# Where an SBUF arena and its parts start: moving the addresses of a three-pass matmul kernel's buffers

## The chip, the cores and the metric

The kernel runs on one core of one Trainium2 chip. The metric is the device time of one execution in microseconds; the time of before is the median of three runs. The profile is of one further execution.

## What is computed

The reference is a stack of two model blocks in float32, on 512 tokens of 1024 features.

```python
def first_block(x, p, ...):                      # DEPTH = 2
    for i in range(2):
        mix = ssd_mixer(x, ...) if i == 0 else hgrn2_mixer(x, ...)   # in-projection, scan over chunks, out-projection
        h = layer_norm(ALPHA * x + mix, ln_g[i, 0], ln_b[i, 0])
        a = relu(h @ w1[i]); h = layer_norm(ALPHA * h + (a * a) @ w2[i], ln_g[i, 1], ln_b[i, 1])
        x = h + sigmoid(h @ w_gate[i]) * (p[i] @ w_proj[i])
    return x
# second block, one layer: x + (concat(mla_attention, memory_attention) * silu(gate)) @ w_out, then rmsnorm
```

w1 is 1024 x 4096 and w2 4096 x 1024, so each of the two MLPs is the largest piece. All projections are products of 512 tokens with 1024 or more features.

## The kernel before, in words

**Arithmetic.** Every large product is made of three passes. An operand is split into a high part, rounded to the fp32r type, and a low part, the difference; TensorE then adds high x high, high x low and low x high into one PSUM bank. The first named operand of a matmul record in the profile is the one that streams (the moving one), the second the one that stands (the stationary one, which a LDWEIGHTS loads): `f_lo,w_hi` streams f_lo over w_hi.

**Stages in order of time.** The SSD mixer by four groups (about 50 to 310 us), its out-projection, MLP 0 (425 to 790), gate 0, the gated recurrence by eight heads (to 1110) with its out-projection, MLP 1 (1200 to 1560), gate 1, the attention layer (to the end). Weights come from HBM in units of 1024 x 512 values as four DMAs on SyncE's queue into one of two slots. ScalarE rounds a unit's slices into w_hi (line 1654, `split_high`), VectorE makes w_lo (line 2432, `split_low`), and TensorE multiplies in `times_parts` (line 907): for each of 8 slices k and 4 blocks c three matmuls of 512 columns, 96 in a unit. Semaphores count the slices; ScalarE may overwrite a slice of w_hi when TensorE is one block on (`blocks_begun`). In the MLP's first product w stands and f streams, in all others of line 907 the activations stand and w streams. Line 702 is `passes`, used by the SSD mixer and others, with in_hi (in fT), in_lo (in res), rings and z_hi (in the arena), x_lo and z_lo (in the slots) and bc_lo (in gb). Line 1081 is the recurrence's projection, 940 the small plain-f32 product with pT, 667 a transpose.

**Memory.** SBUF buffers are allocated one behind the other, each start rounded up to 32 bytes: two slots of 16 KB per partition, res, rn and fT of 16 KB, gb of 8 KB, then the constants, small tiles and pT, then the arena of 29,920 words. The arena is used again in each stage: `carve` hands out views by a running word number, and `part` makes an fp32r tensor at a given word. The parts of the MLP are hid_hi at word 0, f_hi 5632, hid_lo 9728, f_lo 13824, w_hi 17920 and w_lo 22016; all these are multiples of 512 words, 2048 bytes. yT_hi_a, m_hi and first_hi lie in fT.

Of the kernel before, what the change touches and what calls it, by code (L numbers as in the profile page):

```python
# [12 lines left out]
F32R = mybir.dt.float32r  # L13
# [3 lines left out]
P = 128  # L17
T = 512
NT = T // P
D = 1024  # L20
KD = D // P
HALF = 512
NHALF = D // HALF
DEPTH = 2
# [2 lines left out]
RMS_EPS = 1e-5  # L27
EPS = 1e-6
ARENA = 29920
DFF = 4 * D  # L30
KF = DFF // P
PLE = 256
KP = PLE // P
# [17 lines left out]
NMEM = 256  # L51
MT = NMEM // P
# [16 lines left out]
A_CW, A_CB, A_ROWS = 0, TAPS * CONV_BLOCKS, (TAPS + 1) * CONV_BLOCKS  # L69
# [28 lines left out]
    return c  # L98


class Banks:


# [28 lines left out]
def build(nc, x, p, cst, par_a, par_b, w_ssd, w_dt, dt_bias, a_log, d_skip, w_ssd_out, w_hgrn, w_hgrn_out,  # L132
          ln_g, ln_b, w_mlp1, w_mlp2, w_gate, w_proj, mem, pos, w_mla, w_uq, w_ukv, w_mem, w_mla_out, fin_g, out):
    with ExitStack() as ctx:
        def sb(name, shape, dt=F32):
            return ctx.enter_context(nc.sbuf_tensor(name, shape, dt))
# [2 lines left out]
            return ctx.enter_context(nc.semaphore(name))  # L139


        slots = [sb(f"slot{s}", [P, 4096]) for s in range(2)]
        slots_base = nc.sbuf_base - 2 * 4 * 4096
        res = sb("res", [P, NT, D])
# [3 lines left out]
        fT_base = nc.sbuf_base - 4 * KD * T  # L148
        gb = sb("gb", [P, 2, D])
        gb_base = nc.sbuf_base - 4 * 2 * D  # L150
        con = sb("con", [P, C_ALL])
        col_a = sb("col_a", [P, A_ROWS])
        col_b = sb("col_b", [P, B_ROWS])
        eps_h = sb("eps_h", [P, 1])
        pT = sb("pT", [P, DEPTH, KP, T])
        pT_base = nc.sbuf_base - 4 * DEPTH * KP * T
        posi = sb("posi", [P, NT])
        st6 = sb("st6", [P, NT, 2, 6])
        mv = sb("mv", [P, NT, 2])
        ms = sb("ms", [P, NT, 3])  # L160
        arena = sb("arena", [P, ARENA])
        arena_base = nc.sbuf_base - 4 * ARENA
        psum = ctx.enter_context(nc.psum_tensor("psum", [P, 8, HALF], F32))
        tri = con[:, C_TRI:C_TRI + P]
        ones = con[:, C_ONE:C_ONE + P]
# [1 line left out]
        at = [0]  # L167

        def carve(*shape):
            n = int(np.prod(shape))  # L170
            assert at[0] + n <= ARENA, (at[0], n)
            v = arena[:, at[0]:at[0] + n]
            at[0] += n
            if len(shape) == 2:
                v = v.rearrange("p (a b) -> p a b", a=shape[0])
            if len(shape) == 3:
                v = v.rearrange("p (a b c) -> p a b c", a=shape[0], b=shape[1])
            return v


        xdt = carve(NT, HALF)
        xw = carve(NT, HALF)
        xr = carve(NT, HALF)
        zs = carve(NT, HALF)
        prev = carve(NT - 1, HALF)
# [27 lines left out]
        xdt_first, xw_first = 0, 2048  # L213
        dtT = zs[:, 0, :]
        s_par = prev[:, 0, 0:2 * P].rearrange("p (a n) -> p a n", a=2)
        s_p = [arena[:, 26112 + i * NT * PLE:26112 + (i + 1) * NT * PLE].rearrange("p (t n) -> p t n", t=NT)
               for i in range(DEPTH)]
        Mh = rn[:].rearrange("p t d -> p (t d)").rearrange("p (j l) -> p j l", j=S_HPG)
        bc_w = gb[:].rearrange("p a b -> p (a b)").rearrange("p (k n) -> p k n", k=KD)
# [1 line left out]


        def part(name, first, *shape):
            return nc.alloc_sbuf_tensor_at(name, [P, *shape], F32R, offset=arena_base + 4 * first)

        def over(name, base, *shape):
            return nc.alloc_sbuf_tensor_at(name, [P, *shape], F32R, offset=base)
# [2 lines left out]
        bc_lo = over("bc_lo", gb_base, KD, 256)  # L230
        x_lo, z_lo = over("x_lo", slots_base, KD, HALF), over("z_lo", slots_base + 4 * 4096, KD, HALF)
        rings = [part(f"ring{n}", ring_first + n * KD * 256, KD, 256) for n in range(3)]
        z_his = [part(f"z_hi{n}", ring_first + n * KD * 256, KD, HALF) for n in range(2)]
        yT_hi = [over("yT_hi_a", fT_base, KD, T), part("yT_hi_b", 0, KD, T)]
        yT_lo = [part("yT_lo_a", 13824, KD, T), part("yT_lo_b", 9728, KD, T)]
        sums_parts, picks = over("sums_parts", pT_base, T), over("picks", pT_base + 4 * T, S_HEADS)
# [14 lines left out]
        w_hi, w_lo = part("w_hi", 17920, KD, HALF), part("w_lo", 22016, KD, HALF)  # L251
        hid_hi, hid_lo = part("hid_hi", 0, KD, T), part("hid_lo", 9728, KD, T)

        sq = arena[:, 4096:4096 + 3 * T].rearrange("p (a l) -> p a l", a=3)
        sg = arena[:, 9728:9728 + 4096].rearrange("p (t d) -> p t d", t=NT)

        def pp(i, t):

            return pT[:, i, :, :].rearrange("p k l -> p (k l)") if t == NT - 1 else arena[:, 26112 + t * D:26112 + (t + 1) * D]

        first_hi, first_lo = over("first_hi", fT_base, KD, HALF), z_lo

# [60 lines left out]
        ukv_hi, ukv_lo = part("ukv_hi", 17920, KKV, A_HEADS * 2 * NOPE), part("ukv_lo", 22016, KKV, A_HEADS * 2 * NOPE)  # L323
        out_his = [part("out_hi0", 22016, KD, HALF), part("out_hi1", 16384, KD, HALF)]
        branch_lo = part("branch_lo", 0, KD, T)
        mem_tok = arena[:, 0:MT * D].rearrange("p (a b) -> p a b", a=MT)
        memT = arena[:, MT * D:MT * D + KD * NMEM].rearrange("p (a b) -> p a b", a=KD)
        gate = rn


# [1115 lines left out]
        def _(act):  # L1446
# [235 lines left out]
            def projected(stage, i, j):  # L1682

                t, h = j // NHALF, j % NHALF
                b = full(stage, (h, t))
                act.copy(pp(i, t)[:, h * HALF:(h + 1) * HALF], psum[:, b, :]).then_inc(bank_free[b], 1)
# [470 lines left out]
        def _(dve):  # L2157
# [405 lines left out]
            def half_gate(i, h, t):  # L2563

                cols = slice(h * HALF, (h + 1) * HALF)
                wait_taken(dve, f"gate{i}", (h, t))
                dve.wait_ge(res_ready, NT * (2 * i + 1) + t + 1)
                dve.tensor_tensor(sg[:, t, cols], sg[:, t, cols], pp(i, t)[:, cols], ALU.mult)
                dve.drain()
                dve.tensor_tensor(res[:, t, cols], res[:, t, cols], sg[:, t, cols], ALU.add)\  # L2570
                    .then_inc(sig(f"{('ple_first', 'ple_second')[h]}{i}"), 1)
# [585 lines left out]
```

## Time and profile before

| | |
|---|---|
| median of 3 runs | 1894.97 us (1894.18 to 1897.01) |
| span of the profiled execution | 1893.3 us |
| TensorE busy | 1868.5 us, 99% |
| VectorE, ScalarE, GpSimd busy | 1139.9, 921.3, 178.3 us |
| granted TensorE clock, mean | 0.998 |
| DMA | 162.02 MB, 86 GB/s |

The span runs from the first to the last instruction; the time of a run holds a little more. A matmul's record covers its issue, its stream and its drain, so records of one engine overlap, and two matmuls in a row start nearer to each other than a record is long. Names are those of the program's tensors, with buffer numbers left out: `ring` stands for three of them.

### The profile page before, as it was taken

Reading aid. Unit: us, or ns where it says so; the run is one execution under the profiler, and the core shown is the slowest. Engines: PE = TensorE matmul, PEld = TensorE weight load, DVE = VectorE, ACT = ScalarE, POOL = GpSimd, SP = SyncE. Lnnn points to the kernel's source line nnn. Section 1 sums busy time; section 2 is a strip of 40 time slices with the busy share of each in tenths; the row PEclk is TensorE's granted clock in tenths of the full one; section 3 lists DMA queues with packets and bytes.
Section 4 is the critical chain, followed back from the end, with each engine's and each line's share of the span. In section 5 each row is a group of like instructions: output and inputs, shape, how many; then the busy total and the mean of one; then the engine's idle time right before and its main releaser. Section 6 shows DMA issues by size and latency. Waiting matters only on the chain.

```text
span 1893.3 us, 26981 instructions
## 1 busy us (share of the span) xinstructions
PE 1868.5 (99%) x9678; PEld 1573.6 (83%) x9678; DVE 1139.9 (60%) x2013; ACT 921.3 (49%) x1827; POOL 178.3 (9%) x137
## 2 busy tenths in 40 slices
PE   8999999999999999999999999999999999999998
PEld 7787887877888888899999977888888889887986
DVE  5677577548444434557887876634344587456765
ACT  5765765444332323546768655323333364535551
POOL 0201202004000000400101003100000220001100
PEclk9999999999999999999999999999999999999999
DMA  6131214314223322313312124323222222320001
GB/s 199 45 96 42 87 45 153 114 68 156 89 90 113 108 89 89 89 46 90 90 45 67 45 80 143 112 92 117 102 89 89 89 101 92 116 100 1 1 0 45
DMA packets 116738, 162.02 MB, mean 86 GB/s; under 512 B 6085, under 2 KB 57251, under 8 KB 116643
## 3 DMA queue, kind: packets, MB, share of 16 engines
q1 hardware_dynamic: 115347, 156.04, 24.6%
q0 software_dynamic: 1296, 4.72, 0.7%
q8 instruction: 59, 0.97, 0.2%
q14 instruction: 36, 0.29, 0.0%
HBM read 158.64 MB, written 2.10 MB: 85 GB/s over the span
## 4 chain that ended last, share of the span: by engine, by line
PE 92%; DVE 4%; ACT 3%; DVEq 1%; issue 0%; ACTq 0%; DMA 0%; SPq 0%
PE psum L907 52%; PE psum L702 15%; PE psum L1081 8%; PE psum L667 4%; PE psum L1114 3%; PE psum L1344 2%; PE psum L853 1%; PE psum L940 1%; DVE arena L2275 1%; DVE z_lo L2199 1%; PE psum L1001 1%; PE psum L860 1%; PE psum L848 1%; ACT rn L1548 1%; PE psum L1188 0%; ACT arena L1542 0%
## 5 line engine op out<-in xcount | busy, mean ns | idle before, releaser
L2432 DVE TENSOR_TENSOR w_lo<-slot,w_hi 128x512 fp32r<-128x512 f32 x304 | 233.1, 786 | 352.3 <-ACT w_hi L1654 352.2
L1654 ACT CAST w_hi<-slot 128x512 fp32r<-128x512 f32 x304 | 184.5, 620 | 426.9 <-PE psum L907 411.0
L907 PE MATMUL psum<-f_lo,w_hi 128*128 128x512 f32 x528 | 205.8, 390 | 0.0
L907 PE MATMUL psum<-f_hi,w_hi 128*128 128x512 f32 x512 | 200.1, 391 | 1.4 <-DVE f_lo L2480 1.0
L907 PE MATMUL psum<-w_hi,hid_hi 128*128 128x512 f32 x512 | 199.8, 390 | 0.0
L907 PE MATMUL psum<-w_hi,hid_lo 128*128 128x512 f32 x512 | 199.5, 390 | 0.0
L907 PE MATMUL psum<-f_hi,w_lo 128*128 128x512 f32 x512 | 199.5, 390 | 0.0
L907 PE MATMUL psum<-w_lo,hid_hi 128*128 128x512 f32 x512 | 199.4, 390 | 0.0
L3056 POOL TENSOR_TENSOR res<-rn,gb 128x1024 f32<-128x1024 f32 x16 | 46.3, 2892 | 840.1 <-DVE rn L2420 632.6
L907 PEld LDWEIGHTS psum<-f_lo,w_hi 128*128 128x128 f32 x528 | 99.2, 188 | 20.6 <-issue 0.2
L907 PEld LDWEIGHTS psum<-f_hi,w_hi 128*128 128x128 f32 x512 | 96.1, 188 | 22.9 <-DVE f_lo L2480 1.8
L907 PEld LDWEIGHTS psum<-w_hi,hid_hi 128*128 128x128 f32 x512 | 96.2, 188 | 19.9
L907 PEld LDWEIGHTS psum<-w_hi,hid_lo 128*128 128x128 f32 x512 | 96.2, 188 | 19.9
L907 PEld LDWEIGHTS psum<-f_hi,w_lo 128*128 128x128 f32 x512 | 96.2, 188 | 19.9
L907 PEld LDWEIGHTS psum<-w_lo,hid_hi 128*128 128x128 f32 x512 | 96.2, 188 | 19.7
L907 PE MATMUL psum<-w_hi,f_lo 128*128 128x512 f32 (+2 forms) x224 | 83.0, 370 | 0.0
L702 PE MATMUL psum<-in_hi,ring 128*128 128x512 f32 x192 | 77.7, 405 | 0.0
L702 PE MATMUL psum<-in_lo,ring 128*128 128x512 f32 x192 | 75.5, 393 | 0.0
L667 PE MATMUL psum<-con,arena 128*128 128x128 f32 (+1 forms) x486 | 70.4, 274 | 0.4 <-DVE branch_lo L2977 0.3
L2275 DVE SCALAR_TENSOR_TENSOR arena<-psum,col_a,arena 128x511 f32<-128x511 f32 (+2 forms) x72 | 53.4, 748 | 28.7 <-ACT arena L1536 25.1
L1081 PE MATMUL psum<-w_hi,f_hi 128*128 128x256 f32 x224 | 65.7, 293 | 0.0
L667 PEld LDWEIGHTS psum<-con,arena 128*128 128x128 f32 (+1 forms) x486 | 57.7, 146 | 7.4 <-issue 1.9
(388 smaller groups left out, 4385.1 us busy)
## 6 DMA issues: line engine op xcount, KB each, us to landing
slot<-in_w_mlp SPq DMA_DIRECT2D x128, 512.0 KB, 5.7
slot<-in_w_ssd SPq DMA_DIRECT2D x32, 512.0 KB, 5.7
slot<-in_w_hgrn SPq DMA_DIRECT2D x32, 512.0 KB, 6.7
slot<-in_w_ssd_out SPq DMA_DIRECT2D x16, 512.0 KB, 5.9
slot<-in_w_gate SPq DMA_DIRECT2D x16, 512.0 KB, 5.3
gb<-in_w_ssd SPq DMA_DIRECT2D x8, 512.0 KB, 8.3
slot<-in_w_hgrn_out SPq DMA_DIRECT2D x8, 512.0 KB, 5.8
slot<-in_w_mla SPq DMA_DIRECT2D x8, 512.0 KB, 5.4
```

The costliest lines, as they stand in the source:

```text
L667: return pe.transpose(psum[0:mp, b, cols:cols + kp], src, con[0:kp, C_ID:C_ID + kp])
L702: m = pe.matmul(out, a, m_, start=first and n_pass == 0, stop=last and n_pass == 2)
L848: pe.matmul(psum[:, b, :], Btok[:, c, :], xw[:, c, :], start=True, stop=True).then_inc(bank_full[b], 1)
L853: m = pe.matmul(psum[:, b, j * S_P:(j + 1) * S_P], Mh[:, j, c * P:(c + 1) * P], xdt[:, c, j * S_P:(j + 1) * S_P], start=True, stop=True)
L907: m = pe.matmul(psum[:, bank[c], cols or slice(0, width)], a, m_, start=opens and k == 0 and n_pass == 0, stop=closes and k == KD - 1 and ...
L1081: m = pe.matmul(out, a, m_, start=k == 0 and n_pass == 0, stop=k == KD - 1 and n_pass == 2)
L1114: m = pe.matmul(psum[:, b, c * P:(c + 1) * P], a, a, start=True, stop=True)
L1344: m = pe.matmul(psum[:, b, (t - 1) * V_HEAD:t * V_HEAD], probT[:, (t - 1) % 2, c * P:(c + 1) * P], values(c), **first_and_last(c, nk))
L1654: act.copy(w_hi[:, k, :], as_k(slot_of(stage, n))[:, k, :]).then_inc(high_made, 1)
L2275: m = dve.scalar_tensor_tensor(cv[:, n % 3, back:T], psum[:, b, 0:T - back], col_a[:, at_:at_ + 1], cv[:, n % 3, back:T], ALU.mult, ALU.add)
L2432: dve.tensor_tensor(w_lo[:, k, :], as_k(slot_of(stage, n))[:, k, :], w_hi[:, k, :].bitcast(F32), ALU.subtract).then_inc(low_made, 1)
L3056: pool.tensor_tensor(res[:, t, :], rn[:, t, :], gb[:, 0, :], ALU.mult).then_inc(sig("res_scaled"), 1)
```

## The change

The small tiles col_a, posi, st6, mv and ms move to the front of SBUF; pT and then the arena come right behind gb; the constants con, col_b and eps_h go behind the arena. Within the arena, a function `placed` maps a word number to one up to 14 words later, by the table GUARDS, and the arena grows by 14 words. `carve`, `part` and the views written out by hand all use it. As the allocator rounds to 32 bytes, `part` allocates from the multiple of 8 words below and slices. By the table a buffer that starts at word 9728 comes 8 words (32 bytes) later, from 13824 on 12 words (48 bytes), from 22016 on 14 words (56 bytes).

```diff
+GUARDS = ((5632, 0), (9728, 8), (13824, 12), (17920, 12), (22016, 14), (26112, 14))
+ARENA_WORDS = ARENA + GUARDS[-1][1]
+def placed(word):
+    return word + max([guard for first, guard in GUARDS if first <= word], default=0)
+        col_a = sb("col_a", [P, A_ROWS])
+        posi = sb("posi", [P, NT])
+        st6 = sb("st6", [P, NT, 2, 6])
+        mv = sb("mv", [P, NT, 2])
+        ms = sb("ms", [P, NT, 3])
         slots = [sb(f"slot{s}", [P, 4096]) for s in range(2)]
...
         gb = sb("gb", [P, 2, D])
+        pT = sb("pT", [P, DEPTH, KP, T])
+        arena = sb("arena", [P, ARENA_WORDS])
         con = sb("con", [P, C_ALL])
-        col_a = sb("col_a", [P, A_ROWS])
         col_b = sb("col_b", [P, B_ROWS])
         eps_h = sb("eps_h", [P, 1])
-        pT = sb("pT", [P, DEPTH, KP, T])
-        posi = sb("posi", [P, NT])
-        st6 = sb("st6", [P, NT, 2, 6])
-        mv = sb("mv", [P, NT, 2])
-        ms = sb("ms", [P, NT, 3])
-        arena = sb("arena", [P, ARENA])
...
-            v = arena[:, at[0]:at[0] + n]
+            v = arena[:, placed(at[0]):placed(at[0]) + n]
...
         def part(name, first, *shape):
-            return nc.alloc_sbuf_tensor_at(name, [P, *shape], F32R, offset=arena_base + 4 * first)
+            at_, n = placed(first), int(np.prod(shape))
+            whole = nc.alloc_sbuf_tensor_at(name, [P, at_ % 8 + n], F32R, offset=arena_base + 4 * (at_ - at_ % 8))
+            v = whole[:, at_ % 8:at_ % 8 + n]
+            return v.rearrange("p (a b) -> p a b", a=shape[0]) if len(shape) == 2 else v
```

## Rows read from the trace of the kernel before

**Rows 1.** The page: busy time by engine, then the chain by engine and line.
```profile
PE 1868.5 (99%) x9678; PEld 1573.6 (83%) x9678; DVE 1139.9 (60%) x2013; ACT 921.3 (49%) x1827; POOL 178.3 (9%) x137
...
PE 92%; DVE 4%; ACT 3%; DVEq 1%; issue 0%; ACTq 0%; DMA 0%; SPq 0%
PE psum L907 52%; PE psum L702 15%; PE psum L1081 8%; PE psum L667 4%; PE psum L1114 3%; PE psum L1344 2%; PE psum L853 1%; PE psum L940 1%; DVE arena L2275 1%; DVE z_lo L2199 1%; PE psum L1001 1%; PE psum L860 1%; PE psum L848 1%; ACT rn L1548 1%; PE psum L1188 0%; ACT arena L1542 0%
```
**Rows 2.** Waits of TensorE: total us, times, longest.
```profile
PE psum L667 <- DMA rn<-in_x: 5.7, 2, 5.4
```
**Rows 3.** Timeline, TensorE, 800 to 804 us: start, us, instruction (19 matmuls).
```profile
800.12 0.39 PE L907 MATMUL psum<-w_lo,f_hi 128*128 128x512 f32 x1
...
804.20 0.39 PE L907 MATMUL psum<-w_lo,f_hi 128*128 128x512 f32 x1
```
**Rows 4.** Timeline of the weight loads, same stretch.
```profile
800.12 0.19 PEld L907 LDWEIGHTS psum<-w_hi,f_lo 128*128 128x128 f32 x1
```
**Rows 5.** Timeline, TensorE, MLP 0's second product (14 matmuls).
```profile
499.96 0.39 PE L907 MATMUL psum<-w_hi,hid_lo 128*128 128x512 f32 x1
...
502.90 0.39 PE L907 MATMUL psum<-w_hi,hid_hi 128*128 128x512 f32 x1
```
**Rows 6.** Timeline, TensorE, six plain f32 matmuls merged.
```profile
423.57 2.74 PE L940 MATMUL psum<-slot,pT 128*128 128x512 f32 x6
```
**Rows 7.** Timeline, TensorE, SSD out-projection from fT (13 matmuls).
```profile
339.77 0.40 PE L907 MATMUL psum<-w_hi,yT_hi_a 128*128 128x512 f32 x1
...
342.57 0.40 PE L907 MATMUL psum<-w_hi,yT_hi_a 128*128 128x512 f32 x1
```
**Rows 8.** Timeline, TensorE, 256 columns: 19 across buffers, 22 in the arena.
```profile
834.00 0.28 PE L702 MATMUL psum<-f_hi,first_hi 128*128 128x256 f32 x1
...
836.11 0.28 PE L702 MATMUL psum<-f_hi,first_hi 128*128 128x256 f32 x1
...
870.49 0.28 PE L1081 MATMUL psum<-w_hi,f_lo 128*128 128x256 f32 x1
...
873.01 0.28 PE L1081 MATMUL psum<-w_hi,f_lo 128*128 128x256 f32 x1
```
**Rows 9.** Groups by line and shape, TensorE: busy us, mean ns; idle before.
```profile
L907 PE MATMUL psum<-f_lo,w_hi 128*128 128x512 f32 x528 | 205.8, 390 | 0.0
...
L702 PE MATMUL psum<-in_hi,ring 128*128 128x512 f32 x192 | 77.7, 405 | 0.0
L702 PE MATMUL psum<-in_lo,ring 128*128 128x512 f32 x192 | 75.5, 393 | 0.0
...
L702 PE MATMUL psum<-z_hi,in_hi 128*128 128x512 f32 x128 | 50.7, 396 | 0.0
...
L907 PE MATMUL psum<-w_hi,yT_hi_a 128*128 128x512 f32 x64 | 25.9, 405 | 0.3 <-DVE rn L2450 0.3
L702 PE MATMUL psum<-out_hi,m_hi 128*128 128x512 f32 x64 | 25.7, 401 | 0.0
...
L907 PE MATMUL psum<-w_hi,m_hi 128*128 128x512 f32 x64 | 25.6, 400 | 0.0
...
L907 PE MATMUL psum<-w_lo,yT_hi_a 128*128 128x512 f32 x64 | 25.4, 397 | 0.0
```
**Rows 10.** Windows: us, then busy us by engine, clock, DMA share, GB/s.
```profile
425.00:790.00 365.00, 364.53 (x1603) 298.59 (x1602) 179.81 (x257) 128.89 (x231) 34.55 (x15) 1.00 0.29 101
...
880.00:1110.00 230.00, 227.20 (x1605) 209.79 (x1604) 185.53 (x335) 160.56 (x337) 20.27 (x16) 0.99 0.20 56
```
**Rows 11.** Waits of all engines: total us, times, longest.
```profile
ACT w_hi L1654 <- PE psum L907: 411.0, 203, 2.1
```
**Rows 12.** The page: costliest groups of VectorE and ScalarE, and the MLP's DMAs.
```profile
L2432 DVE TENSOR_TENSOR w_lo<-slot,w_hi 128x512 fp32r<-128x512 f32 x304 | 233.1, 786 | 352.3 <-ACT w_hi L1654 352.2
L1654 ACT CAST w_hi<-slot 128x512 fp32r<-128x512 f32 x304 | 184.5, 620 | 426.9 <-PE psum L907 411.0
...
slot<-in_w_mlp SPq DMA_DIRECT2D x128, 512.0 KB, 5.7
```

More of the change, by code:

```diff
@@ L150, in build @@
         gb_base = nc.sbuf_base - 4 * 2 * D
+        pT = sb("pT", [P, DEPTH, KP, T])
+        pT_base = nc.sbuf_base - 4 * DEPTH * KP * T
+        arena = sb("arena", [P, ARENA_WORDS])
+        arena_base = nc.sbuf_base - 4 * ARENA_WORDS
         con = sb("con", [P, C_ALL])
-        col_a = sb("col_a", [P, A_ROWS])
         col_b = sb("col_b", [P, B_ROWS])
         eps_h = sb("eps_h", [P, 1])
-        pT = sb("pT", [P, DEPTH, KP, T])
-        pT_base = nc.sbuf_base - 4 * DEPTH * KP * T
-        posi = sb("posi", [P, NT])
-        st6 = sb("st6", [P, NT, 2, 6])
-        mv = sb("mv", [P, NT, 2])
-        ms = sb("ms", [P, NT, 3])
-        arena = sb("arena", [P, ARENA])
-        arena_base = nc.sbuf_base - 4 * ARENA
         psum = ctx.enter_context(nc.psum_tensor("psum", [P, 8, HALF], F32))
@@ L215, in build @@
         s_par = prev[:, 0, 0:2 * P].rearrange("p (a n) -> p a n", a=2)
-        s_p = [arena[:, 26112 + i * NT * PLE:26112 + (i + 1) * NT * PLE].rearrange("p (t n) -> p t n", t=NT)
+        s_p = [arena[:, placed(26112) + i * NT * PLE:placed(26112) + (i + 1) * NT * PLE].rearrange("p (t n) -> p t n", t=NT)
                for i in range(DEPTH)]
@@ L252, in build @@
         hid_hi, hid_lo = part("hid_hi", 0, KD, T), part("hid_lo", 9728, KD, T)
-        sq = arena[:, 4096:4096 + 3 * T].rearrange("p (a l) -> p a l", a=3)
-        sg = arena[:, 9728:9728 + 4096].rearrange("p (t d) -> p t d", t=NT)
+        sq = arena[:, placed(4096):placed(4096) + 3 * T].rearrange("p (a l) -> p a l", a=3)
+        sg = arena[:, placed(9728):placed(9728) + 4096].rearrange("p (t d) -> p t d", t=NT)
         def pp(i, t):
-            return pT[:, i, :, :].rearrange("p k l -> p (k l)") if t == NT - 1 else arena[:, 26112 + t * D:26112 + (t + 1) * D]
+            return pT[:, i, :, :].rearrange("p k l -> p (k l)") if t == NT - 1 else arena[:, placed(26112) + t * D:placed(26112) + (t + 1) * D]
         first_hi, first_lo = over("first_hi", fT_base, KD, HALF), z_lo
@@ L325, in build @@
         branch_lo = part("branch_lo", 0, KD, T)
-        mem_tok = arena[:, 0:MT * D].rearrange("p (a b) -> p a b", a=MT)
-        memT = arena[:, MT * D:MT * D + KD * NMEM].rearrange("p (a b) -> p a b", a=KD)
+        mem_tok = arena[:, placed(0):placed(0) + MT * D].rearrange("p (a b) -> p a b", a=MT)
+        memT = arena[:, placed(MT * D):placed(MT * D) + KD * NMEM].rearrange("p (a b) -> p a b", a=KD)
         gate = rn
```

## The prediction

> **What bounds the kernel now.** I read the page first: TensorE is busy for 1868.5 of the span's 1893.3 us, and the chain that ended last runs through it for 92% of the time, 52% on line 907 alone [rows 1]. Then the waits of TensorE: the list of them adds up to under 20 us, and its first is 5.7 us for the first rows of x [rows 2]. No other engine holds it up: VectorE has 60% of the span and ScalarE 49%. So the time is the number of matmuls times their pitch, the distance from one start to the next, and the question is only what the change does to that pitch.
>
> The records hide the pitch, because a matmul's 390 ns hold its drain too. It has to be read in the timeline. In the first gate's product (weights stream, activations stand), 18 steps go from 800.12 to 804.20 us: 226.7 ns each [rows 3], and the load of the next matmul's stationary operand starts with the matmul that streams, at 800.12 [rows 4]. In the MLP's product with w2, 13 steps go from 499.96 to 502.90: 226.2 ns [rows 5]. At the full clock (the granted share was 1.00 in every MLP stretch, and 2.4 GHz is that level) 512 columns take 213.3 ns. So each of these matmuls loses 13.3 ns, about 6%. Is that loss a fixed cost, or something the addresses decide? Three places tell.
>
> First, plain f32 matmuls on line 940, whose operands also lie in SBUF and whose weights are reloaded each time: six take 2.74 us, the last one with its 0.593 us record, so the pitch is (2740 - 593)/5 = 429 ns, against 426.7 for 512 columns at half rate [rows 6]. Loss: under 3 ns. A weight load beside a slow stream costs nearly nothing.
>
> Second, line 907 again, the same three-pass form with the same shapes, but the activations' high part in fT instead of in the arena: 12 steps from 339.77 to 342.57 are 233.3 ns each [rows 7]. The only thing that differs is which addresses are read. Adding the sizes in the source, each rounded to 32 bytes (the constants' 5696, col_a 480, col_b 416, eps_h 32, pT 8192, posi 32, st6 192, mv 32, ms 64), the arena stands 800 bytes behind slots, res, rn, fT and gb modulo 2048. Within the arena every part that TensorE reads starts at a multiple of 2048 from its start. So "same address modulo 2048" is 226.7 and "800 off" is 233.3.
>
> Third, the 256-column form: in the arena, 21 steps from 870.49 to 873.01 give 120.0 ns, 13.3 over 106.7, the same loss per weight load as at 512 columns; with the gate projection's weights in fT and slots, 18 steps from 834.00 to 836.11 give 117.2 ns [rows 8]. There a different distance is better than equal addresses by 2.8 ns. The loss is therefore per weight load, it is moved by the relative address, and the equal address is not its minimum.
>
> Grouped by shape, the records say the same, because record = pitch + 163 ns in both cases (390 and 226.7; 593 and 429): the arena's own pairs stand at 390 to 391 (six groups of 512 or 528, of which one is shown), pairs across buffers at 392 to 405 [rows 9].
>
> **The change part by part.**
>
> *Same address modulo 2048.* The small tiles col_a, posi, st6, mv, ms (480 + 32 + 192 + 32 + 64 = 800 bytes) now stand ahead of slots, and the constants, col_b and eps_h (5696 + 416 + 32 = 6144 = 3 x 2048) behind the arena; pT is 4 x 2048. Every large buffer gets the arena's old phase. That does nothing to pairs inside the arena. What it can give back is the excess over 390 of the pairs across. By groups [rows 9]: in_hi,ring 192 x 15 ns, in_lo,ring 192 x 3, z_hi,in_hi 128 x 6, yT_hi_a 64 x (15 + 7), w_hi,m_hi 64 x 10, out_hi,m_hi 64 x 11: 2.9 + 0.6 + 0.8 + 1.4 + 0.6 + 0.7 = 7.0 us. A dozen smaller groups of the same view, 32 to 160 matmuls each at 391 to 397, add some 4. The groups of 400 to 405 hold a few short waits, which stay, so of these 11 I take 8.5 us. The 256-column gate projection loses its lucky distance: 192 x 2.8 ns = 0.5 us. Net gain 8 us. Ends: 0 (the offsets spoil it) and 11.
>
> *The offsets (placed, part).* Counted from the arena's start: parts below word 9728 (hid_hi, f_hi, yT_hi_b, o_hi) stay; hid_lo and yT_lo_b come 32 bytes later, f_lo, yT_lo_a and o_lo 48, w_hi, ring 0 and 1 and z_hi 48, w_lo 56. In the product with w1 a stream of f_hi (0) now runs beside a load of w_hi (48), and one of f_lo (48) beside a load of w_lo (56); in the product with w2 w_hi (48) beside hid_hi (0), w_lo (56) beside hid_lo (32). Distances from stream to load thus become +48, +8, -48, -24 where all were 0. The trace of before has no such distance: its allocator's 32-byte steps show only 0 and 32 modulo 64. So I bound it from both sides. Best: all of the 13.3 ns goes. Line 907 has 528 + 5 x 512 = 3,088 of these in its six large groups [rows 9]; with the smaller groups of 702, 907, 1001 and 1081 some 6,900 fp32r matmuls follow one another directly, 4,700 of them with all operands in the arena. So 6,900 x 13.3 = 92 us, or 76 us if 2.3 ns stay as in the f32 row [rows 6]. Worst: the arena's pairs fall to what pairs across show, 233.3 - 226.7 = 6.6 ns [rows 3, 7], on the 4,700: +31 us. The nearest rows of a distance that is better than 0 are the 256-column ones, 2.8 ns a load [rows 8], and their distance is 32 modulo 64. I take 4.2 ns, between those 2.8 and half of the 13.3, because the offsets reach all four kinds of pair: 6,900 x 4.2 = 29 us.
>
> The first group of stages (SSD, 310 us) gets it in part only: in_hi and in_lo both stay at 0, as do bc_lo, x_lo and z_lo; this is inside the 29.
>
> *The rest.* `part` makes the same views with another start; no instruction is added or removed on any engine, and DMA issues stay the same. ScalarE's split (620 ns) and VectorE's (786 ns) write to w_hi and w_lo at the new starts [rows 12]. Should these get slower by a tenth, 8 of each per unit would take 1.1 us more beside a unit of 96 x 226.7 ns = 21.8 us of TensorE in which VectorE is busy half the time (179.81 of 365 us) [rows 10]: hidden. What is late next if TensorE gains 2%: ScalarE's split waits for it, 411.0 us in all [rows 11], and VectorE's for ScalarE's; a unit's four DMAs land in a median of 5.7 us against 21.8 [rows 12]. Nothing there turns into a wait. The stage with least cover is the recurrence from 880 to 1110 us, VectorE 185.53 of 230 [rows 10]; a wait there could keep some 1 us of the gain.
>
> **A rule that speaks against this.** The two ways of reading the same SBUF differ by 6.6 ns a matmul [rows 3, 7]. The Trainium skill, "TensorE: Matmul & The Clock Gate", section "Step-by-step: what each phase is for", says that TensorE has two independent read ports and that loading the next weights takes no bandwidth from the running matmul. By that rule addresses would decide nothing and the sum would be 0; the trace disagrees, with 226.7, 233.3 and 117.2 against 120.0. The skill's "SBUF — State Buffer", section "Door 1: The DMA port swizzle", has lines of 16 bytes and a penalty for each crossing; 56 is no multiple of 16, so by this rule of the Trainium skill the streams of w_lo cross one line more, and a little is lost, not gained (the last rival's direction). No row here shows such a start.
>
> **The sum.** 1893.3 - 8 - 29 = 1856 us of span. The profiled execution's span stands 1.7 us below the median of the three runs (1894.97), the rest being what lies around it; 1856 + 2 = 1858 us, 2% faster.
>
> **The rivals.**
> - *The offsets take nearly all of the loss.* Pitches fall to about 217 ns, as in the f32 row's remainder of 2 to 3 ns. For: the loss is exactly the same at 256 and 512 columns, so it is one thing that a right distance could end. Against: no stretch of a fast stream is under 117 ns at 256 columns or under 226 at 512. Price: 76 + 8, so 1811 us.
> - *Only the alignment counts.* The offsets are as good as 0. For: 0 already is the best of the 512-column rows. Then 8 us: 1887.
> - *No change*: the loss is fixed and the differences have another cause, for instance which engine writes beside it; or the changed pairs gain what the arena's lose. 1895 us. Against: within a group the pitch repeats to 1 ns while other engines come and go.
> - *Slower: the starts off the 64-byte grid cost more than equal addresses do.* Every stream and load that is moved takes extra reads, and every arena pair comes to the pitch of the pairs across. +31 - 8 = +23 us: 1918. It decides from the point where the arena's 4,700 pairs lose what alignment gives: 8/4,700 = 1.7 ns, a pitch over 228.4. For: both distances off 0 that 512-column rows show (32 modulo 64, either sign) are worse. Against: the 256-column row.
>
> **How the numbers follow.** The forecast, 1835 to 1880, gets 0.62; nearly all of the loss gone, 0.12; alignment only, 0.08; no change, 0.07; slower, 0.11. What a measurement here can tell from no change is 0.2%, 3.8 us. Faster 0.82, same 0.07, slower 0.11. The range 1818 to 1897 leaves out the slower case and the best half of the first rival, 0.17 together.
>
> **What would show it.** In the timeline of the changed kernel the same stretch of the MLP should have pitches near 222 ns instead of 226.7, records near 386 instead of 390 in all six groups of 907; yT_hi_a, m_hi and in_hi groups should lose more than the arena's groups. TensorE stays at 99% busy with the same waits. Weight loads keep their 188 ns. If the six groups stand at 390, the offsets do nothing; at 380, the loss was all collision; above 392, the slower rival holds. If TensorE's waits grow by more than 5 us, the cover reckoned above was wrong.

## The result, and the profile after

The changed kernel takes 1916.22 us (1914.91 to 1916.8), the kernel before 1894.58 beside it on the same chip: a ratio of 1.0111, interval 1.0098 to 1.0125. So it is 1.1% slower, 21.6 us, where 2% faster was forecast. Its profiled span is 1914.3 us, 21.0 more than before, so the profile holds nearly all of the difference.

The page of the kernel after, busy time by engine and the chain by engine, beside [rows 1]:

```profile
PE 1889.8 (99%) x9678; PEld 1574.3 (82%) x9678; DVE 1139.6 (60%) x2013; ACT 922.2 (48%) x1827; POOL 178.9 (9%) x137
...
PE 92%; DVE 3%; ACT 3%; DVEq 1%; issue 0%; ACTq 0%; DMA 0%; SPq 0%
```

Every count is the same. TensorE is busy 21.3 us longer, and that is the 21.0 us of the span. Weight loads, VectorE, ScalarE and GpSimd stand within 1 us of before. TensorE waits no longer either: all its waits add up to 17.2 us, as before. It is the matmuls themselves. Which ones, the groups by line and shape tell (line 907 of before is 918 now, 702 is 713, 1081 is 1092), beside [rows 9]:

```profile
L918 PE MATMUL psum<-f_lo,w_hi 128*128 128x512 f32 x528 | 207.8, 394 | 0.0
L918 PE MATMUL psum<-f_hi,w_hi 128*128 128x512 f32 x512 | 204.1, 399 | 1.4 <-DVE f_lo L2491 1.0 <-ACT pT L1697 0.5
L918 PE MATMUL psum<-w_lo,hid_hi 128*128 128x512 f32 x512 | 203.6, 398 | 0.0
L918 PE MATMUL psum<-f_hi,w_lo 128*128 128x512 f32 x512 | 202.5, 395 | 0.0
L918 PE MATMUL psum<-w_hi,hid_lo 128*128 128x512 f32 x512 | 202.3, 395 | 0.0
L918 PE MATMUL psum<-w_hi,hid_hi 128*128 128x512 f32 x512 | 200.9, 392 | 0.0
L713 PE MATMUL psum<-in_hi,ring 128*128 128x512 f32 x192 | 77.7, 405 | 0.0
L713 PE MATMUL psum<-in_lo,ring 128*128 128x512 f32 x192 | 75.7, 394 | 0.0
```

The six large groups went from 390 or 391 to 392 to 399, each to its own value. The pairs across buffers, which the alignment should have mended, stand where they stood (405 and 394). The pitch itself is in the timeline. Product with w2, the stretch of [rows 5], first and last of 13 starts (start us, record us, engine, instruction):

```profile
500.12 0.39 PE L918 MATMUL psum<-w_hi,hid_hi 128*128 128x512 f32 x1
...
502.91 0.39 PE L918 MATMUL psum<-w_hi,hid_hi 128*128 128x512 f32 x1
```

12 steps in 2.79 us are 232.5 ns; before they were 226.2. Product with w1, the same view:

```profile
455.15 0.40 PE L918 MATMUL psum<-f_hi,w_hi 128*128 128x512 f32 x1
...
457.97 0.40 PE L918 MATMUL psum<-f_hi,w_hi 128*128 128x512 f32 x1
```

12 steps, 235.0 ns. And one window with both MLP products in it, 425 to 790 us, beside [rows 10] (us, then busy us and count for TensorE, weight loads, VectorE, ScalarE, GpSimd; clock, DMA share, GB/s):

```profile
425.00:790.00 365.00, 364.54 (x1556) 291.34 (x1555) 173.25 (x247) 120.94 (x215) 32.38 (x14) 1.00 0.29 101
```

1,556 matmuls instead of 1,603 in the same 365 us, with TensorE just as full and its clock at the upper level in both: 2.9% fewer, as a pitch of 233 instead of 226.7 would give. For the whole trace there is a sum: for each fp32r matmul of lines 702, 907, 1001 and 1081 with n columns, the distance from its start to the next one's less n/2.4 ns (the time of n columns at 2.4 GHz), with distances of more than 40 ns over that left out as waits. It is 101.4 us before and 123.8 after, +22.4, over some 6,850 matmuls in each. That is the loss to explain.

### The profile page after: what moved, and what is told of

The parts are those of the page before. It is cut to its first block, busy times and chain, and to the rows that moved or that the text cites. A ratio compares the mean times of both kernels' runs of the same rounds, so it can differ in the third digit from the quotient of the medians.

```text
span 1914.3 us, 26981 instructions
## 1 busy us (share of the span) xinstructions
PE 1889.8 (99%) x9678; PEld 1574.3 (82%) x9678; DVE 1139.6 (60%) x2013; ACT 922.2 (48%) x1827; POOL 178.9 (9%) x137
## 4 chain that ended last, share of the span: by engine, by line
PE 92%; DVE 3%; ACT 3%; DVEq 1%; issue 0%; ACTq 0%; DMA 0%; SPq 0%
PE psum L918 52%; PE psum L713 15%; PE psum L1092 8%; PE psum L678 4%; PE psum L1125 3%; PE psum L1355 2%; PE psum L864 1%; PE psum L951 1%; DVE arena L2286 1%; DVE z_lo L2210 1%; PE psum L1012 1%; PE psum L871 1%; PE psum L859 1%; ACT rn L1559 1%; PE psum L1199 0%; ACT arena L1553 0%
## 5 line engine op out<-in xcount | busy, mean ns | idle before, releaser
L2443 DVE TENSOR_TENSOR w_lo<-slot,w_hi 128x512 fp32r<-128x512 f32 x304 | 233.6, 786 | 370.3 <-ACT w_hi L1665 370.1
L1665 ACT CAST w_hi<-slot 128x512 fp32r<-128x512 f32 x304 | 184.9, 620 | 446.2 <-PE psum L918 429.9
L918 PE MATMUL psum<-f_hi,w_hi 128*128 128x512 f32 x512 | 204.1, 399 | 1.4 <-DVE f_lo L2491 1.0
L918 PE MATMUL psum<-w_lo,hid_hi 128*128 128x512 f32 x512 | 203.6, 398 | 0.0
L918 PEld LDWEIGHTS psum<-w_hi,hid_lo 128*128 128x128 f32 x512 | 96.6, 189 | 21.3
```

The costliest lines, as they stand in the source:

```text
L918: m = pe.matmul(psum[:, bank[c], cols or slice(0, width)], a, m_, start=opens and k == 0 and n_pass == 0, stop=closes and k == KD - 1 and ...
L1665: act.copy(w_hi[:, k, :], as_k(slot_of(stage, n))[:, k, :]).then_inc(high_made, 1)
L2443: dve.tensor_tensor(w_lo[:, k, :], as_k(slot_of(stage, n))[:, k, :], w_hi[:, k, :].bitcast(F32), ALU.subtract).then_inc(low_made, 1)
```

## Experiments

The base of each diff is the changed kernel, where nothing else is said. A guard `(first, words)` moves all parts from word `first` on by so many words of 4 bytes.

**1. The alignment without the offsets.**

```
-GUARDS = ((5632, 0), (9728, 8), (13824, 12), (17920, 12), (22016, 14), (26112, 14))
+GUARDS = ((5632, 0), (26112, 0))
```

> The changed kernel with every offset in GUARDS set to 0: the large buffers stay at one address modulo 2048. Theory A (the offsets inside the arena do the harm, the alignment helps): the arena's six groups of line 918 go back to records of 390 ns, the pairs across buffers come down to 390 to 392 too, and the time is 1894.6 - 8 = 1886 to 1888 us. Theory B (equal addresses across different buffers are no gain, the loss across had another cause): 1894 to 1896 us, pairs across stay at 394 to 405.

Measured: 1888.41 us (before 1895.58), ratio 0.9962, interval 0.9949 to 0.9976. Groups of TensorE:

```profile
L918 PE MATMUL psum<-f_lo,w_hi 128*128 128x512 f32 x528 | 205.4, 389 | 0.0
L918 PE MATMUL psum<-f_hi,w_hi 128*128 128x512 f32 x512 | 199.8, 390 | 1.4 <-DVE f_lo L2491 1.0 <-ACT pT L1697 0.5
...
L713 PE MATMUL psum<-in_hi,ring 128*128 128x512 f32 x192 | 77.0, 401 | 0.0
L713 PE MATMUL psum<-in_lo,ring 128*128 128x512 f32 x192 | 74.8, 389 | 0.0
```

The alignment alone gains 7.2 us, and the sum over the starts falls from 101.4 to 93.5 us. Most pairs across come to 389 or 390, but in_hi,ring only from 405 to 401: where one of its matmuls directly follows another the pitch is 227 ns in the median, so most of what is left in the mean is short waits. So the offsets cost the whole of 1916.22 - 1888.41, some 28 us.

**2. The offsets without the alignment:** buffers allocated in the order of before, the guards kept.

```
-        col_a = sb("col_a", [P, A_ROWS])
...
         slots = [sb(f"slot{s}", [P, 4096]) for s in range(2)]
...
         gb = sb("gb", [P, 2, D])
...
+        con = sb("con", [P, C_ALL])
+        col_a = sb("col_a", [P, A_ROWS])
...
         arena = sb("arena", [P, ARENA_WORDS])
-        con = sb("con", [P, C_ALL])
```

> The old order of buffers (the arena 800 bytes behind the slots, res, rn, fT and gb modulo 2048) with the offsets of GUARDS inside the arena. Theory A (harm and help add): the changed kernel's 1916 us plus the 8 us that alignment would give, 1922 to 1926 us. Theory B (alignment gives nothing): the same as the changed kernel, 1914 to 1918 us. In both the six groups of line 907 in the MLPs stand at the changed kernel's 392 to 399 ns, as these pairs lie within the arena.

Measured: 1917.14 us, ratio 1.0112 (1.0097 to 1.0127). The offsets by themselves make the whole loss: beside the kernel before of its own session this one is 21.6 us slower, just as the changed kernel is. So the alignment, worth 7 us alone, is worth at most 1 us beside the offsets, which these runs can't tell from nothing. The expected 1922 to 1926 of theory A added the two as if they were independent. They aren't: with the offsets in, most pairs across are off one another either way. The 1914 to 1918 of theory B came, but its reason is refuted by experiment 1.

**3. Distances, but all starts on multiples of 64 bytes.**

```
+GUARDS = ((5632, 0), (9728, 16), (17920, 32), (22016, 48))
```

> The changed kernel with offsets that are multiples of 64 bytes: low activations (from word 9728) 64 bytes later, high weights 128, low weights 192. Theory A (only the distance modulo 64 counts): as good as no offsets, 1886 to 1888 us, records of 390 ns. Rival (any distance off 0 modulo 2048 or 512 costs): 1905 us or more and records of 393 to 399 ns.

Measured: 1915.19 us, ratio 1.0105 (1.0089 to 1.012). The six groups:

```profile
L918 PE MATMUL psum<-f_lo,w_hi 128*128 128x512 f32 x528 | 207.5, 393 | 0.0
L918 PE MATMUL psum<-f_hi,w_lo 128*128 128x512 f32 x512 | 203.2, 397 | 0.0
L918 PE MATMUL psum<-w_hi,hid_lo 128*128 128x512 f32 x512 | 203.2, 397 | 0.0
```

Distances of 64 to 192 bytes cost as much as the change does. A theory by which only the distance modulo 64 counts is out, and so is one by which only starts off the 64-byte grid do.

**4. Every pair of starts by itself:** a kernel of its own, with buffers for the stream (m_a to m_h, starts 0, 8 .. 56 bytes) and for the stationary operand (s_a to s_h, the same), and far_a to far_f at 128, 256, 384, 512, 1024 and 1536 bytes; 24 matmuls a pair, 512 columns.

```
r = pe.matmul(psum[:, 0, :], s[:, j * 128:j * 128 + 128], m[:, j % 2 * 512:j % 2 * 512 + 512],
              start=k == 0, stop=k == n - 1)
```

> Not the computation: a kernel that only runs fp32r matmuls of 512 columns, 24 for each pair of a moving buffer that starts 0, 8, ..., 56 bytes (m_a to m_h) and a stationary one that starts 0, 8, ..., 56 bytes (s_a to s_h) behind a multiple of 2048, then m_a with stationary buffers 128, 256, 384, 512, 1024 and 1536 bytes behind. It leaves out all of the reference's work. Theory A (the distance modulo 64 decides): the pitch is 226.7 ns wherever both letters are equal and for all six far buffers, and 228 to 240 ns elsewhere, the same along each diagonal. Rival (each operand's own start decides: off 16, 32 or 64 bytes it costs extra reads): m_a with s_a is lowest, equal letters other than a cost 2 to 10 ns more, and the costs of row and column add.

Pitches in ns by the timeline, the mean of a pair's steps without the first two (down: start of the stream; across: start of the stationary buffer, which is both loaded and standing). Each pair ran once, with the granted clock at 1.00, the upper level:

| | 0 | 8 | 16 | 24 | 32 | 40 | 48 | 56 |
|-|-|-|-|-|-|-|-|-|
| 0 | 226.7 | 230.7 | 233.4 | 230.0 | 233.4 | 233.2 | 233.3 | 233.3 |
| 16 | 231.8 | 231.2 | 231.1 | 233.3 | 236.8 | 232.0 | 226.7 | 233.3 |
| 32 | 233.4 | 231.1 | 228.4 | 233.3 | 227.1 | 230.7 | 233.4 | 230.0 |
| 48 | 230.0 | 232.5 | 232.3 | 226.8 | 231.6 | 233.3 | 233.3 | 233.1 |

The four rows left out (8, 24, 40, 56) lie between 230.9 and 236.5. The groups of this kernel, with records that are 163 ns above the pitch:

```profile
L75 PE MATMUL psum<-m_f,s_d 128*128 128x512 f32 x24 | 5.8, 399 | 0.0
...
L75 PE MATMUL psum<-m_a,far_c 128*128 128x512 f32 x24 | 5.8, 395 | 0.0
L75 PE MATMUL psum<-m_a,far_a 128*128 128x512 f32 x24 | 5.7, 395 | 0.0
...
L75 PE MATMUL psum<-m_a,far_b 128*128 128x512 f32 x24 | 5.6, 390 | 0.0
L75 PE MATMUL psum<-m_e,s_e 128*128 128x512 f32 x24 | 5.6, 390 | 0.0
...
L75 PE MATMUL psum<-m_c,s_g 128*128 128x512 f32 x24 | 5.6, 389 | 0.0
```

No pair is under 226.7, and both theories failed as they were put. What holds: equal starts at 0 or 32 are at the floor, equal starts at 8, 16, 24, 40, 48 or 56 are not (230.9 to 233.3); a distance of 512 is as good as 0 (226.9) and one of 256 comes to 226.7 after its first steps (227.9 with them; 226.7 in experiment 8), one of 128 or 384 is not (232.4). Two pairs, 16 with 48 and 48 with 24, are at the floor without my knowing why.

**5. The start alone:** the whole arena 16 bytes later, all distances within it 0.

```
+GUARDS = ((0, 4), (26112, 4))
```

> The aligned kernel (no offsets) with the whole arena 16 bytes later, so that distances inside the arena stay 0 but every start leaves the 32-byte grid. In the grid, equal letters gave 226.7 (a), 230.9 (b), 231.1 (c) and 233.3 ns (d). Theory C (a start off the grid costs by itself, some 4.4 ns for 16 bytes): 4,700 pairs x 4.4 = 21 us, and more across buffers, 1908 to 1916 us, records of 394 to 395 ns in the MLPs. Rival (in the kernel only distances count): 1888 to 1892 us with records of 390 ns.

Measured: 1910.31 us (before 1894.85), ratio 1.0088 (1.0071 to 1.0104).

```profile
L918 PE MATMUL psum<-f_lo,w_hi 128*128 128x512 f32 x528 | 207.0, 392 | 0.0
...
L918 PE MATMUL psum<-w_hi,hid_hi 128*128 128x512 f32 x512 | 201.1, 393 | 0.0
```

All six groups at 392 or 393 (394 to 395 were expected), the pitch 230.4 to 230.8, where experiment 4 had 231.1 for (16, 16). A start 16 bytes off the 32-byte grid costs 4 ns a matmul without any distance.

**6 and 7. The low weights 256, and 128 bytes later.**

```
+GUARDS = ((5632, 0), (22016, 64))     # 6
+GUARDS = ((5632, 0), (22016, 32))     # 7
```

Experiment 6 also has ARENA at 29904 instead of 29920, so the constants behind the arena start 64 bytes later than in experiment 7.

> The aligned kernel with the low weights (everything from word 22016) 256 bytes later. Theory D (the good distances are the multiples of 256 bytes, as far_b, far_d, far_e and far_f in the grid say against far_a and far_c): as good as no offset, 1888 us within 2 us. Rival (only multiples of 512 or 2048 are good): 1895 us or more, f_lo,w_hi and w_lo,hid_hi records above 391 ns.

> The same with 128 bytes instead of 256, so that the two kernels differ in nothing but that distance. Theory D: the loads of w_lo beside f_lo and those of hid_lo and f_lo beside w_lo rise by 4 to 8 ns on every third matmul of line 918 and its neighbours, with some of it on the matmul behind: 1896 to 1904 us. Rival (64 bytes is the period, and the kernel with 64, 128 and 192 was slow for its 64 and 192 alone): 1888 us.

Measured: 1889.43 us for 256 bytes, ratio 0.9973 (0.9963 to 0.9982), all six groups at 389 or 390 as in experiment 1; 1905.67 us for 128, ratio 1.0059 (1.0042 to 1.0076), a little above what was expected. With 128:

```profile
L918 PE MATMUL psum<-f_lo,w_hi 128*128 128x512 f32 x528 | 209.2, 396 | 0.0
L918 PE MATMUL psum<-f_hi,w_lo 128*128 128x512 f32 x512 | 203.3, 397 | 0.0
L918 PE MATMUL psum<-w_lo,hid_hi 128*128 128x512 f32 x512 | 202.3, 395 | 0.0
L918 PE MATMUL psum<-f_hi,w_hi 128*128 128x512 f32 x512 | 199.9, 390 | 1.4 <-DVE f_lo L2491 1.0 <-ACT pT L1697 0.5
L918 PE MATMUL psum<-w_hi,hid_hi 128*128 128x512 f32 x512 | 199.8, 390 | 0.0
L918 PE MATMUL psum<-w_hi,hid_lo 128*128 128x512 f32 x512 | 198.9, 389 | 0.0
```

Just half of the groups pay. w_lo,hid_hi streams the moved weights beside operands at 0. f_hi,w_lo streams from 0 over the moved weights, which stand. f_lo,w_hi has nothing moved of its own, but the load of w_lo runs beside it. The other three have distance 0 both to what stands and to what is loaded. So it is the distance within a pair that costs, not the place of a buffer, and the rows fit a reading in which both the standing and the loaded operand count. That reading is an inference: no run moved one of the two alone.

**8. The distance in steps of 32 bytes,** the stream at 0, the load (d_a to d_q) at 0 to 512, with 512 and with 256 columns; then loads of one word 128 times, and of 64 and 32 columns.

```
wide:      mov[:, j % 2 * 512:j % 2 * 512 + 512]
half:      mov[:, j % 4 * 256:j % 4 * 256 + 256]
one word:  s[:, j * 128:j * 128 + 1].broadcast_to([P, P])
```

> Not the computation: fp32r matmuls only, all of them streaming one buffer (stream) that starts at a multiple of 2048, with stationary buffers d_a to d_q that start 0, 32, ..., 512 bytes behind one; first 512 columns, then 256 columns, then with a stationary operand that reads one word 128 times, then with 64 and with 32 stationary columns instead of 128. It leaves out all of the reference's work. Theory D: pitch 226.7 ns at distances 0, 256 and 512, 229 to 236 between. Theory E (the loss is collision with the load, so it goes with the words that the load reads): 13.3 ns at 128 stationary columns, about 7 at 64 and 3 at 32, and 0 to 3 with the one word; pitch never under 226.7 with 128 columns at any distance. Rival (the loss is a fixed cost of changing weights): 226 ns or more in all of them.

The timeline, 24 matmuls to a row, so that the pitch is about the row's second number less 0.39 us (0.28 at 256 columns), over 23. The granted clock was 1.00 in all of them:

```profile
39.53 5.75 PE L68 MATMUL psum<-stream,d_b 128*128 128x512 f32 x24
...
67.54 5.67 PE L68 MATMUL psum<-stream,d_g 128*128 128x512 f32 x24
...
78.64 5.61 PE L68 MATMUL psum<-stream,d_i 128*128 128x512 f32 x24
84.08 5.75 PE L68 MATMUL psum<-stream,d_j 128*128 128x512 f32 x24
...
128.63 3.03 PE L75 MATMUL psum<-stream,d_a 128*128 128x256 f32 x24
...
137.17 2.98 PE L75 MATMUL psum<-stream,d_d 128*128 128x256 f32 x24
...
176.97 5.72 PE L82 MATMUL psum<-stream,d_a 128*128 128x512 f32 x24
...
226.92 5.85 PE L89 MATMUL psum<-stream,d_b 128*32 128x512 f32 x24
```

The table leaves out the first three steps of each row, in which some pairs are slower; by the whole row distance 192 has 229.6:

| distance | 0 | 32 | 64 | 96 | 128 | 160 | 192 | 224 | 256 |
|-|-|-|-|-|-|-|-|-|-|
| 512 columns | 226.7 | 233.3 | 233.3 | 234.4 | 233.3 | 233.4 | 228.8 | 233.3 | 226.7 |
| 256 columns | 120.0 | 118.2 | 117.8 | 117.3 | 118.8 | 120.0 | 117.8 | 117.9 | 119.7 |

From 256 to 512 both rows repeat. This is the row that the prediction lacked: at 512 columns 0 (with 256 and 512) is the best distance and everything else is worse, at 256 columns 0 is about the worst. The 233.3 at 32 and at 224 is the 233.3 of [rows 7]: there stream and load are 800 bytes apart, 3 x 256 + 32, one way or the other. One word loaded 128 times costs 231.7 at each of the four distances run, also at 0, where 128 different words cost 226.7. Nor do 64 columns (229.3 to 232.7) or 32 (230.7 to 238.5) instead of 128 cost less. So the loss doesn't go with the number of words loaded, and theory E is out. The rival, 226 ns or more in all of them, came out as put: a fixed cost of changing weights stays possible for the 13.3 ns, though not for what the distance adds.

**9. The kernel before with 224 bytes of padding,** no buffer reordered.

```
-ARENA = 29920
+ARENA = 29904
...
+        sb("pad_a", [P, 8])
         pT = sb("pT", [P, DEPTH, KP, T])
...
+        sb("pad_b", [P, 48])
         arena = sb("arena", [P, ARENA])
```

> The kernel before with two unused tiles put in (32 bytes ahead of pT, 192 ahead of the arena; the arena 16 words shorter, which nothing used): the arena then stands 1024 bytes behind the slots modulo 2048 instead of 800, and pT 512 instead of 480, all multiples of 256; nothing else moves. Theory D (the distance modulo 256 decides): as good as the aligned kernel, 1887 to 1890 us. Rival (equal addresses modulo 2048 are needed across buffers): 1893 to 1895 us.

Measured: 1889.33 us (before 1895.62), ratio 0.9967 (0.9955 to 0.9979), and the group of f_lo,w_hi at 389 as in experiment 1, that of in_hi,ring at 401. Equal addresses modulo 256 do; modulo 2048 isn't needed. Experiments 1, 6 and 9 beat both kernels, and their intervals don't part them.

**10. The kernel's own triples in isolation, and other widths.** Sets of four buffers at the starts that the kernel gives them (up: product with w1; down: with w2; low and all: experiments 7 and 5), 16 rounds of the three passes, no other engine at work.

```
for q, (a, m) in enumerate(((s_hi, m_hi), (s_hi, m_lo), (s_lo, m_hi))):
    r = pe.matmul(psum[:, 1, :], a[:, j * 128:j * 128 + 128], m[:, j % 2 * 512:j % 2 * 512 + 512],
```

> Not the computation: fp32r matmuls only, all reference work left out. First one pair at distance 0 with 512, 448, 384, 320, 288, 256, 192 and 128 columns; then the three-pass order (high, low, high streamed over high, high, low standing) for six sets of starts: even (all 0), up and down (the changed kernel's MLP products: 0, 48 over 48, 56 and 48, 56 over 0, 32), low and far (the last part 128 or 256 bytes later), all (each part 16 bytes later). Theory F (starts alone make the changed kernel's pitch, no other engine's access has part in it): even 226.7 ns, up 233 to 234, down 232 to 233, low 229 to 231, far 226.7, all 229.5 to 231; and a loss of 13.3 ns at every width of 192 columns and more. Rival (the writes of VectorE and ScalarE beside it make part of it): up and down within 2 ns of even.

```profile
L80 PE MATMUL psum<-down_mlo,down_shi 128*128 128x512 f32 x16 | 6.4, 397 | 0.0
L80 PE MATMUL psum<-up_mhi,up_shi 128*128 128x512 f32 x16 | 6.4, 397 | 0.0
...
L80 PE MATMUL psum<-down_mhi,down_slo 128*128 128x512 f32 x16 | 6.3, 395 | 0.0
...
L80 PE MATMUL psum<-down_mhi,down_shi 128*128 128x512 f32 x16 | 6.3, 392 | 0.0
...
L80 PE MATMUL psum<-up_mlo,up_shi 128*128 128x512 f32 x16 | 6.2, 389 | 0.0
L80 PE MATMUL psum<-far_mhi,far_shi 128*128 128x512 f32 x16 | 6.2, 389 | 0.0
```

Down: 228.7, 235.3 and 233.5 ns, in the kernel's product with w2 229.0, 235.2 and 233.6. The addresses alone make these, to 0.3 ns. Up: 234.3, 226.7, 232.3, a mean of 231.1, where 233 to 234 were expected; the kernel's product with w1 has 235.7, 230.0, 234.1, a mean of 233.3. The other sets: even comes to 227.0 after its first steps, far has 226.7, low 231.3 and all 230.1, as expected or nearly so.

The 2.2 ns that are left over with w1 have a pattern. The product runs in eight stretches of 192 matmuls, the same three passes at the same addresses, and each keeps to one of two levels: mean pitches of 235.5, 231.1, 235.4, 231.1 in MLP 0 and 235.4, 231.1, 235.4, 231.1 in MLP 1. The lower level is what the set has in isolation. Beside the 235.0 of 455.15 to 457.97 us above, first and last of 13 starts in the second stretch:

```profile
541.87 0.40 PE L918 MATMUL psum<-f_hi,w_hi 128*128 128x512 f32 x1
...
544.64 0.40 PE L918 MATMUL psum<-f_hi,w_hi 128*128 128x512 f32 x1
```

12 steps, 230.8 ns. Experiment 2's kernel, with the same offsets, has 231.1 in the first stretch, where the changed kernel has 235.5, and DMA moved about as much in both (155 and 147 GB/s from 440 to 480 us). So off equal addresses the addresses don't settle the pitch alone: four stretches x 192 x 4.4 ns = 3.4 us of the change's loss are a second level, whose cause no run shows. With equal addresses (experiments 1, 6, 9 and the kernel before) all eight stretches are at 226.7 to 227.0.

Distance 0, by width: 512 columns lose 13.3 ns (226.6), with no other engine at work. 448 lose 16.0, 384 13.8, 320 13.3, 288 11.9, 256 13.3, so theory F's 13.3 at every width is right only roughly. At 192 and 128 columns the pitch is the same (111.6 and 111.5), so there it isn't the stream that sets it; what does isn't shown.

## Why the prediction was wrong

**What bounds the kernel: right.** The time is the matmuls' pitch. TensorE's 21.3 us more are the span's 21.0, and seven other ways of placing the buffers moved pitch and time together.

**The alignment, -8 us (0 to 11): right in the sum.** Experiment 1 has -7.2, experiment 9 -6.3. The split was too generous to in_hi,ring: of its 15 ns over 390, 4 were excess and 11 mostly short waits, 0.8 us instead of 2.9. By the sum over starts the gain is where it was looked for: the six large groups of line 907 stay (41.3 to 41.1 us), the smaller groups of 702, 907 and 1001 fall from 45.5 to 37.3, and the 256-column ones lose the 0.5 us that was forecast. That the offsets could spoil it was the lower end, and they do: at most 1 us is left (experiment 2). One reading was a little off: uq_lo starts at word 8064, which is no multiple of 2048 bytes, but only 36 matmuls stream it.

**The offsets, 6,900 x 4.2 ns = -29 us: the step that failed.** Experiment 1 to the changed kernel is +28 us, 4.1 ns on 6,900 matmuls, or 6.0 ns on the arena's 4,700; by the sum over starts, which has 30.3 us for it, 19.1 are on the six large groups, 10.0 on the smaller groups, 2.4 on the recurrence's 512-column ones, and 1.4 gained at 256 columns. The sign was wrong; that the size agrees is chance, as 4.2 was a value chosen between two bounds. "Worst" of that step, 6.6 ns on 4,700 = +31, was the right row to go by. It was passed over on two inferences:
- *"There a different distance is better than equal addresses ... and the equal address is not its minimum."* True at 256 columns, and carried over to 512 because the loss is 13.3 ns at both. Experiment 8 shows that the two widths have different best distances, and experiment 10 that the loss isn't 13.3 at all widths. In the kernel too: the recurrence's 256-column matmuls went from 120.0 [rows 8] to 117 or 118 ns with the offsets, a gain of about 1 us beside the kernel before, and the 512-column ones lost 23.
- *The loss of 13.3 ns as something to be won.* In none of the 64 pairs, 17 distances and six sets at 512 columns was the mean loss less (to 0.1 ns). At 512 columns it is a floor, reached with equal addresses; nearly all other addresses in these runs add to it.

The evidence that argued the other way stood in the prediction, under the slower rival: "both distances off 0 that 512-column rows show ... are worse". Rows of the same width as the 6,900 matmuls should have weighed more than rows of another.

**The rest: right.** Of VectorE's and ScalarE's splits at the new starts, beside [rows 12], the page after says:

```profile
L2443 DVE TENSOR_TENSOR w_lo<-slot,w_hi 128x512 fp32r<-128x512 f32 x304 | 233.6, 786 | 370.3 <-ACT w_hi L1665 370.1
L1665 ACT CAST w_hi<-slot 128x512 fp32r<-128x512 f32 x304 | 184.9, 620 | 446.2 <-PE psum L918 429.9
```

786 and 620 ns as before; only ScalarE's wait for TensorE grew, from 411.0 to 429.9 us [rows 11], since TensorE is slower.

The f32 matmuls of [rows 6] kept their pitch too. Eight of them in the timeline after:

```profile
419.32 3.60 PE L951 MATMUL psum<-slot,pT 128*128 128x512 f32 x8
```

With a record of 0.592 us for the last, (3600 - 592)/7 = 430 ns, though slot and pT came from 480 bytes apart, modulo 2048, to 0. At half rate this distance isn't felt.

**The rule on read ports.** By the Trainium skill ("TensorE: Matmul & The Clock Gate", section "Step-by-step: what each phase is for") TensorE has two independent read ports and a load takes nothing from the running matmul. The kernel before already disagreed with that; experiment 8 makes it plain, 226.7 to 234.4 ns by nothing but the stationary buffer's address. The 16-byte lines of the Trainium skill ("SBUF — State Buffer", section "Door 1: The DMA port swizzle") don't explain it either: by them a start 16 bytes off crosses no line more, and experiment 5 lost 4 ns a matmul by it.

**The slower rival was the case that came.** Its price was +31 - 8 = +23 against +21.6 measured. Its threshold held: all six groups passed a pitch of 228.4 (the lowest, w_hi,hid_hi, has 229.0), and five of them passed a record of 392, with the sixth at 392. That the price is so near is luck in part: beside the kernel before all pairs together lost 22.4 us where it has 31, and the alignment gave next to nothing beside the offsets where it has 8 (experiment 2), and the two misses cancel. Its reason held in half: starts off a grid do cost (experiment 5; the grid is 32 bytes, since (32, 32) is at 227.1), but distances on the 64-byte grid cost as much (experiment 3). Its chance of 0.11 was too low.

**What stays open.** Why the floor is 13.3 ns, and by what mechanism the distance adds to it. Ruled out: writes by other engines as the main part (experiment 10), and a loss that goes with the number of words loaded (experiment 8). No stream without a load beside it was run, so I can't say that the floor comes from the load. What puts a stretch of the product with w1 on the level of 235.5 ns or on that of 231.1 isn't shown, and neither is why experiment 5's kernel has 231.1 in MLP 0 and 230.0 in MLP 1.

## What to carry to other kernels

Where fast matmuls with 512 columns reload their stationary operand each time, put every buffer that TensorE reads, streams and loads alike, at a multiple of 256 bytes from the others and on the 32-byte grid. Here 224 bytes of padding gave 0.3%, and offsets of 32 to 56 bytes cost 1.5%. Read the effect from the distance of starts, at the width that the kernel uses: 256 columns told the opposite of 512. And before a pattern is extended to where no row stands, one small grid of the sizes in question settles it.

## What the runs showed of the hardware

- The pitch of 512 columns depends on the distance from the stream to the stationary buffer (loaded and standing) with a period of 256 bytes: 226.7 ns at 0, 256 and 512, 228.8 at 192, 233.3 to 234.4 at the others (experiment 8).
- Equal addresses are not enough: with both starts at 8 to 24 bytes off the 32-byte grid the pitch is 230.9 to 233.3 (experiment 4), and 230.4 to 230.8 in the whole kernel at 16 (experiment 5).
- At 256 columns the best distance is 96 (117.3 ns), and 0 and 160 are the worst (120.0; experiment 8).
- A load of fewer columns (32 or 64), or of one word repeated, takes nothing off the pitch of the stream beside it: 229.3 to 238.5 ns (experiment 8), never under 226.7.
- Off equal addresses the same three passes at the same addresses can run at two levels, each kept for a stretch of 192 matmuls: 231.1 and 235.5 ns in the changed kernel's product with w1.
